# Layer 0 of a hybrid encoder: 14 of 62 depthwise taps as ScalarE products, summed by accumulating DMAs

## The reference

```python
h = modulate(rms_norm(x, norm1_g[l]), sh1, sc1)
z = h @ w_in[l]
za, zb, zq, zk, zv = jnp.split(z, split_idx, axis=-1)
ya = conformer_conv(za, ...)    # 256 channels, 31 taps
yb = short_gated_conv(zb, ...)  # 256 channels, 3 taps
yc = diff_attention(zq, zk, zv, ...)  # 4 heads
mix = jnp.concatenate([ya, yb, yc], axis=-1) @ w_out[l]
x = x + g1[:, None, :] * mix

def conformer_conv(za, conv_w, conv_b, norm_g):
    val, gate = jnp.split(za, 2, axis=-1)
    u = val * jax.nn.sigmoid(gate)
    u = depthwise_conv(u, conv_w, conv_b)
    return jax.nn.silu(rms_norm(u, norm_g))
```

## Time and profile before

| what | us |
|---|---|
| median of 3 runs | 1187.54 (1187.3 to 1188.18) |
| span of the profiled execution, first to last instruction | 1186.5 |
| PE busy | 1175.3 |
| VectorE busy | 728.5 |
| ScalarE busy | 506.8 |
| GpSimd busy | 119.3 |
| 62 taps of layer 0 and 62 of layer 1: 120 of them on L1229 | 83.7 |

### The profile page before, as it was taken

The page is one execution under the profiler, slowest core; times in us unless marked ns, Lnnn a source line. Parts: engine busy times, 40 slices in busy tenths (PEclk is TensorE's granted clock), DMA queues, the critical chain, the costliest instruction groups (busy, mean ns, idle before and its releaser), DMA issues.

```text
span 1186.5 us, 14451 instructions
## 1 busy us (share of the span) xinstructions
PE 1175.3 (99%) x5168; PEld 929.8 (78%) x5168; DVE 728.5 (61%) x1056; ACT 506.8 (43%) x768; POOL 119.3 (10%) x195
## 2 busy tenths in 40 slices
PE   9999999999999999999999999999999999999998
PEld 6787556878888888888888876678888888888887
DVE  7989998985556432577478998757733333332221
ACT  5546788463222232322234468866523232332220
POOL 2321232211012000121000112100000000000000
PEclk9999999999999999999999999999999999999999
DMA  8777346986565323697323764423332323223332
GB/s 302 249 240 178 80 96 197 307 264 212 186 199 170 106 89 106 227 314 256 106 89 102 165 142 94 85 54 107 107 106 88 106 89 98 96 93 105 105 104 88
DMA packets 48940, 175.18 MB, mean 148 GB/s; under 512 B 5697, under 2 KB 5825, under 8 KB 48898
## 3 DMA queue, kind: packets, MB, share of 16 engines
q1 hardware_dynamic: 30386, 107.13, 27.7%
q0 software_dynamic: 18512, 67.51, 20.4%
HBM read 172.52 MB, written 2.10 MB: 147 GB/s over the span
## 4 chain that ended last, share of the span: by engine, by line
PE 84%; DVE 10%; ACT 4%; issue 2%; DVEq 0%; ACTq 0%; POOL 0%; POOLq 0%
PE ps L1699 22%; PE ps L1700 22%; PE ps L1701 22%; PE ps L1728 3%; DVE uc L1229 3%; PE ps L1765 2%; PE ps L1767 2%; PE ps L1766 2%; PE ps L1732 2%; ACT prob L783 1%; PE ps L1970 1%; DVE neg_max L1333 1%; PE ps L1747 1%; PE ps L1755 1%; PE ps L1748 1%
## 5 line engine op out<-in xcount | busy, mean ns | idle before, releaser
L644 ACT ACTIVATE w_hi<-raw 128x1024 fp32r<-128x1024 f32 x196 | 207.5, 1060 | 519.7 <-PE ps L1701 465.7
L1041 DVE TENSOR_TENSOR w_lo<-raw,w_hi 128x1024 fp32r<-128x1024 f32 x164 | 201.5, 1228 | 240.6 <-ACT w_hi L644 238.5
L1699 PE MATMUL ps<-h_hi,w_hi 128*128 128x512 f32 x832 | 329.0, 395 | 0.0
L1701 PE MATMUL ps<-h_lo,w_hi 128*128 128x512 f32 x832 | 324.1, 390 | 0.0
L1700 PE MATMUL ps<-h_hi,w_lo 128*128 128x512 f32 x832 | 324.1, 389 | 0.0
L1699 PEld LDWEIGHTS ps<-h_hi,w_hi 128*128 128x128 f32 x832 | 156.2, 188 | 48.5 <-issue 17.3
L1701 PEld LDWEIGHTS ps<-h_lo,w_hi 128*128 128x128 f32 x832 | 156.2, 188 | 32.8
L1700 PEld LDWEIGHTS ps<-h_hi,w_lo 128*128 128x128 f32 x832 | 156.3, 188 | 31.2 <-issue 0.5
L1699 PE MATMUL ps<-gu_hi,w_hi 128*128 128x512 f32 x352 | 136.9, 389 | 0.0
L1700 PE MATMUL ps<-gu_hi,w_lo 128*128 128x512 f32 x352 | 136.9, 389 | 0.0
L1701 PE MATMUL ps<-gu_lo,w_hi 128*128 128x512 f32 x352 | 136.9, 389 | 0.0
(11 more groups left out here) (225 smaller groups left out, 1408.9 us busy)
## 6 DMA issues: line engine op xcount, KB each, us to landing
raw<-w_stream SPq DMA_DIRECT2D x196, 512.0 KB, 3.4
w_lo<-w_stream POOLq DMA_DIRECT2D x32, 512.0 KB, 7.9
ada_ring_gu<-ada POOLq DMA_DIRECT2D x28, 512.0 KB, 4.3
ada_ring_late<-ada POOLq DMA_DIRECT2D x28, 512.0 KB, 5.0
ada_ring_first<-ada POOLq DMA_DIRECT2D x16, 512.0 KB, 5.0
ada_ring_mid_a<-ada POOLq DMA_DIRECT2D x12, 512.0 KB, 5.0
ada_ring_mid_b<-ada POOLq DMA_DIRECT2D x12, 512.0 KB, 4.9
xT<-x_t SPq DMA_DIRECT2D x4, 512.0 KB, 5.6
```

The costliest lines, as they stand in the source:

```text
L644: act.activation(w_hi[:, u % RING, :], raw[:, u % RAW, :], ACT.Copy).then_inc(s_whi, 1)
L1041: dve.tensor_tensor(w_lo[:, u % RING, :], raw[:, u % RAW, :], w_hi[:, u % RING, :].bitcast(F32), ALU.subtract).then_inc(s_wlo, 1)
L1699: pe.matmul(dst, whi, rhs[0][:, n, :], start=start, stop=False)
L1701: return pe.matmul(dst, whi, rhs[1][:, n, :], start=False, stop=stop)
```

## The change

Seven tap positions of the 31 (the last seven), in both chunks, are taken from DVE in layer 0. ACT makes their products `ua` x weight, 128x512 each: the first of each chunk goes into `tap_sum`, the others into six slots of `tap_product`. POOL adds them onto `tap_sum` by accumulating DMAs inside the chip's SBUF, 256 KB each, twelve in all, in pairs between the weight additions. Two more accumulating DMAs add `tap_sum` onto `uc` (`add_tap_sums`, issued in tile 11). In tile 12 DVE waits for them before it squares. The buffers lie in the region of `ada_ring_mid_a`, so that ring's first four loads are issued in tile 12, behind the last of these DMAs.

```diff
+SCALAR_TAPS = 7
+TAP_SLOTS = 6
+VECTOR_TAPS = (CC * (TAPS_A - SCALAR_TAPS), N_TAPS)
-TAPS_TILE = ((4, 3, 3, 3, 0, 3, 3, 3, 3, 2, 1, 3, 3, 0, 0, 0), ...
+TAPS_TILE = ((2, 2, 2, 2, 0, 2, 2, 2, 2, 2, 2, 0, 0, 0, 0, 0), ...
+ADD_BEHIND = (U_V, U_V + 1, U_V + 3, U_B + 1, U_B + 2)
...
+            def add_products(n):
+                for c in range(CC):
+                    r = CC * n + c
+                    pool.wait_ge(s_atap, r + 1)
+                    if n > 1:
+                        pool.wait_ge(s_tadd[c], 16 * (n - 1))
+                    pool.dma_start(tap_sum[:, c, :], tap_product[:, (r - CC) % TAP_SLOTS, :],
+                                   accum_op=ALU.add).then_inc(s_tadd[c], 16)
+            def add_tap_sums():
+                pool.wait_ge(s_tap, VECTOR_TAPS[0])
+                for c in range(CC):
+                    pool.wait_ge(s_tadd[c], 16 * (SCALAR_TAPS - 1))
+                    pool.dma_start(uc[:, c, :], tap_sum[:, c, :], accum_op=ALU.add).then_inc(s_tmerge[c], 16)
...
+                    if l == 0 and it == CONV_SQUARE_AT - 1:
+                        add_tap_sums()
+                    if l == 0 and it == CONV_SQUARE_AT:
+                        for c in range(CC):
+                            pool.wait_ge(s_tmerge[c], 16)
+                        for m in range(M_MID, M_MID + 4):
+                            ada_load(m)
...
             pool.wait_ge(s_acc, M_MID)
-            for m in range(M_MID, M_MID + 4):
-                ada_load(m)
+            add_products(1)
             for u in range(U_V, U_B + RING):
                 add_raw(u)
+                if u in ADD_BEHIND:
+                    add_products(2 + ADD_BEHIND.index(u))
...
+            def tap_products(first, end):
+                for r in range(first, end):
+                    n, c = divmod(r, CC)
+                    j = TAPS_A - SCALAR_TAPS + n
+                    if n == 0:
+                        act.wait_ge(s_ua, CC)
+                        act.wait_ge(s_pad, 4)
+                        dst = tap_sum[:, c, :]
+                    else:
+                        dst = tap_product[:, (r - CC) % TAP_SLOTS, :]
+                        if r - CC >= TAP_SLOTS:
+                            act.wait_ge(s_tadd[c], 16 * (n - TAP_SLOTS // CC))
+                    act.activation(dst, ua[:, c, j:j + T], ACT.Copy,
+                                   scale=pcol[:, 0, ...]).then_inc(s_atap, 1)
...
                 qk_square(l, 0)
+                if l == 0:
+                    tap_products(0, 6)
                 qk_rstd(l, 0)
                 for s in range(U_Q, U_V):
                     step(U + s)
+                    if l == 0 and s == U_Q + 1:
+                        tap_products(6, 10)
+                    if l == 0 and s == U_Q + 2:
+                        tap_products(10, 12)
                 qk_square(l, 1)
+                if l == 0:
+                    tap_products(12, CC * SCALAR_TAPS)
                 qk_rstd(l, 1)
...
             def conv_square(l):
-                dve.wait_ge(s_tap, N_TAPS * (l + 1))
+                dve.wait_ge(s_tap, sum(VECTOR_TAPS[:l + 1]))
                 for z in range(CC):
+                    if l == 0:
+                        dve.wait_ge(s_tmerge[z], 16)
                     dve.tensor_tensor(mix_sq(z), uc[:, z, :], uc[:, z, :], ALU.mult).then_inc(s_csq, 1)
```

More of the change, by code:

```diff
@@ L123 @@
 TAPS_INPUT, TAPS_BETWEEN = (2, 0), (0, 6)
-TAPS_TILE = ((4, 3, 3, 3, 0, 3, 3, 3, 3, 2, 1, 3, 3, 0, 0, 0), (3, 2, 2, 2, 0, 2, 2, 2, 2, 1, 0, 2, 1, 0, 0, 0))
+TAPS_TILE = ((2, 2, 2, 2, 0, 2, 2, 2, 2, 2, 2, 0, 0, 0, 0, 0), (3, 2, 2, 2, 0, 2, 2, 2, 2, 1, 0, 2, 1, 0, 0, 0))
 QUARTERS = (1, 2, 1, 1, 2, 1, 2, 1, 2, 1, 2, 1, 1, 1, 1, 0)
@@ L276, in encoder_kernel @@
         c_row, _ = place("c_row", [1, D], at=spare_base)
+        tap_sum, tap_end = place("tap_sum", [P, CC, T], at=spare_base)
+        tap_product, tap_end = place("tap_product", [P, TAP_SLOTS, T], at=tap_end)
+        assert tap_end <= at
         q_lo, k_lo_at = place("q_t_lo", [P, HEADS, T], F32R, at=spare_base)
@@ L410, in encoder_kernel @@
         s_tap = sem("taps")
+        s_atap = sem("tap_product")
+        s_tadd = [sem(f"tap_product_added{i}") for i in range(CC)]
+        s_tmerge = [sem(f"tap_sum_added{i}") for i in range(CC)]
         s_short = sem("short_conv_step")
@@ L848, in y_hi @@
                     act.activation(h_hi[:, z, :], src, ACT.Copy).then_inc(s_yhi, 1)
+            def tap_products(first, end):
[11 more added lines that the diff above has]
+                    act.activation(dst, ua[:, c, j:j + T], ACT.Copy,
+                                   scale=pcol[:, 0, C_WA + c * TAPS_A + j:C_WA + c * TAPS_A + j + 1]).then_inc(s_atap, 1)
             act.wait_ge(s_cps, 1)
@@ L1227, in conv_a_taps @@
                     else:
-                        dve.wait_ge(s_tap, N_TAPS * l + i - 1)
+                        dve.wait_ge(s_tap, VECTOR_TAPS[0] * l + i - 1)
                         dve.scalar_tensor_tensor(uc[:, c, :], ua[:, c, j:j + T], w, uc[:, c, :], ALU.mult,
@@ L1527, in _ @@
                         split_lo(U + U_B + STEP_AT[it] + RING)
-                assert taps_done[l] == N_TAPS
+                assert taps_done[l] == VECTOR_TAPS[l]
                 def dots(first, end):
```

## The result

The changed kernel takes 1193.82 us (1192.58 to 1194.28, 4 runs) against 1187.68 for the kernel before: ratio 1.0049, 95% interval 1.0037 to 1.006. It is 6.1 us slower; 4.0 were forecast. Timed again beside later experiments it took 1192.73 against 1187.78, ratio 1.0039 (1.0025 to 1.0052), 5.0 us. In the profiled executions the spans differ by 1191.6 - 1186.5 = 5.1 us.

A forecast was written before the change was run, and what follows sets the result against it. PE bounds, busy 1175.3 of 1186.5 us. The late merge shifts the last statistic by 4.0 us, the 1.3 gain already inside: span 1190.5, median 1.0 above it, so 1191.5 us; range 1186.0 to 1196.5.

The forecast's parts named there:

- PE's waits cap the gain: Layer 0's attention: four PE waits for DVE sum to 1.86 us, all a lighter DVE can return; tiles gain 1.3.
- The merge decides: Tiles 11 to 12: DVE waits for two merging DMAs, landed 181.7 and 183.3; last statistic at 196.15, 4.0 us later.
- Products on ScalarE at 0: Projections: fourteen ACT products of 0.71 us fit into ACT's waits before rstds and behind projection steps; cost nothing.
- From the squares to the last statistic: Layer 0's attention end: 13.24 us before, less 1.0 of ACT's wait, so 12.25 us.
- Side work: Projections: twelve adding DMAs, 1.6 us each, leave weights just in time; taken as 0, bounds 0 and +1.5.
- PE standing before a value unit: Projections: a sign named for the forecast being wrong, PE waiting at a value unit; no size given.
- Queued behind the waiting squares: DVE, tile 12: tile 14's row maximum and inverse and tile 13's mixing wait, holding ACT and PE, tiles 13 to 15.
- Moved loads at 0: Four modulation loads go from 61 us to behind the merge, wanted some 12 us after it; cost nothing.
- rival 2: Projections: additions also starve PE of weights, third to fifth unit 1 to 2 us late; +7, 1194.5; chance 0.11.
- the forecast's own range: Whole kernel: 1189.8 to 1194.2 us, from a merge at 181.5 to 184.5 and 0 to 1.5 in the projections.
- Order in the queue: POOL's queue, tile 11: descriptors go in ring order, so the merge cannot pass the 512 KB weight addition ahead.
- The median's distance from the span: Whole kernel: the median of the runs lies 1.0 us above the profiled span, start and end untouched.

The follow-up runs named there:

- merge in front: Changed kernel with the two merging DMAs issued ahead of tile 11's weight addition instead of behind it: 1187.76 us, ratio 1.0000.
- filler: Changed kernel with 20 small matmuls on PE ahead of its wait for the conformer squares: 1192.03 us, ratio 1.0035; repeated, 1191.88, ratio 1.0036.
- A pair later: Kernel in which VectorE does the merge, seven positions, third pair of adding DMAs behind the third weight addition instead of the second: 1188.97 us, ratio 1.0008.

## Why the prediction was right, step by step

- **PE's waits cap the gain.** Right. Forecast -1.3 for the tiles, with 0.25 left in tile 5; the trace has 0.25 left there, and leaving out the taps gave -1.3 in the traces lined up and -1.6 by the medians.
- **The merge decides.** Right: landings forecast at 181.7 and 183.3, seen at 181.7 and 182.9; squares done 183.9, seen 183.6; PE's standing from 179.4, seen from 179.4. The experiments with the merge in front and on VectorE each took the loss away. That it fits so closely is partly luck: the merge's 1.6 us was half the price of another kind of addition, and in the repeat with filler the same two DMAs took 7.6 and 8.3 us from issue to landing instead of 8.9 and 9.6.
- **Products on ScalarE at 0.** Right: counted from the split near 76 us, the second rstd comes when it did before (20.5 us behind it in both). Not in the prediction: from the ninth product on they wait for slots that the additions free. That cost nothing here; in "A pair later" it cost PE 1.42 us.
- **From the squares to the last statistic: too small.** Forecast 12.25 us, seen 197.35 - 183.6 = 13.75. The term lacks the clock. I had let PE come to a wait of over 4 us and then go on at full speed; the statistic took 3.54 us instead of 1.7, and ScalarE's rstd, which I had expected to lose its wait, waited 1.26 us. Where the clock stayed up (filler, merge in front) the term measured 12.1. With this 1.5 us the 4.0 become 5.5, which is what the lined-up trace of the change shows (5.9 in its repeat, with 0.8 of side work); 6.1 and 5.0 were measured by the medians.
- **Side work: taken at 0, is 0.1 to 1.5.** By itself it was timed at 1.2. The bounds were 0 and +1.5, and the place was named, the third weight addition just in time at 98.4 us: PE waits there for 0.3 to 0.4 us in most executions, the change's repeat among them, though not in the change's first trace. So one of the signs that I had named for being wrong, PE standing before a value unit, did come, at a small price. Not seen by me: SP's raw units, which share the engines and arrive late, near 104 to 106 us. The pairs weigh more than 3.2 us: the second weight addition took 12.8 us to land, 3.8 more than before.
- **Queued behind the waiting squares.** Right as a list, but it is not what set the time: with the clock low, PE had enough work of its own from the statistic on to wait for none of it, and moving the squares behind the row maximum changed nothing.
- **Moved loads at 0.** Right as far as traces show: not tested by itself, but from the last statistic to the end all executions take the same time to 0.2 us.
- **The time itself** doesn't decide between the forecast (1191.5) and rival 2 (1194.5), and 1193.82 lies nearer to the rival. The experiments do: rival 2 asked for 3 us from PE starving in the projections, where 0.1 and 0.8 were seen in the change's two traces. (The low end of the forecast's own range comes to 1189.7, not 1189.8.)
- **Order in the queue** held at the merge: it landed 1.3 us behind the weight addition ahead of it. It is no full picture: with the merges in front, the second took 7.8 us though only the first merge had been issued ahead of it in that place. By the formula of the Trainium skill (DMA: Bandwidth & Descriptors, section "Anatomy of one DMA"), 2.0 us plus bytes over 436 GB/s, 256 KB would take 2.6 us, an estimate; the traces do not agree, 4.2 us for the fastest merge.
- The median's distance from the span, taken as 1.0 us, was that between two different executions: where an execution's span and time are both known it is 1.8. Differences are not touched by it.

## What to carry to other kernels

Before work is moved off an engine, sum the waits of the bounding engine for it: 9.2 us off VectorE were worth 1.6 (1.3 in the traces), and six taps of fourteen gave nearly all of that. A result that comes back through a DMA queue needs its consumer placed by landing time, behind whatever is queued ahead and beside it; check every in-order engine for what stands behind the one that waits, the bounding engine first, since a block that is taken off one queue can stand in the next. In this kernel TensorE's waits of 4.1 to 4.6 us cost 1.2 to 1.7 us more than their length, as the clock was low behind them; a wait of 0.66 us left it at full. And line up two traces at a point ahead of the change before reading a difference of 1 us: here their starts alone differed by up to 0.9.

## What was not expected of the hardware

TensorE's granted clock fell to half during a wait of 4.42 us and was at half for the first 4 us and more of the work behind it (184 to 188 us), in a kernel that otherwise runs at full clock. How long it stays low is not the same each time: in the repeat, after 4.59 us of standing, the mean of 188 to 190 us was 1.00, where it was 0.68 in the first trace. 20 small matmuls in the wait kept it at 1.00. A 256 KB accumulating DMA inside the chip took 4.2 us from issue to landing with the 512 KB raw load issued 1.1 us behind it. The next, issued 0.6 us later, took 7.8 us with that load and the 512 KB weight addition beside it.
